# The first unit of the first projection from products of X that is weighted but not normed yet, and seven more convolution taps on TensorE

## The reference

```python
h = rmsnorm(x, norm_mix[0])            # x * rsqrt(mean(x*x) + eps) * g, per token
u = h @ w_pw1 + b_pw1                  # 1024 -> 2048
a, gate = split(u, 2); u = a * sigmoid(gate)
u = causal_depthwise_conv(u, w_dw, width=31) + b_dw
u = silu(layernorm(u, ln_g, ln_b))
x = x + (u @ w_pw2 + b_pw2)
```

## Time and profile before

| | |
|---|---|
| median of 3 runs | 1744.0 us (1743.5 to 1745.08) |
| profiled execution | 1744.05 us |
| its span | 1742.2 us, mean granted TensorE clock 0.996 |
| TensorE busy | 1713.0 us, 98% |
| VectorE busy | 1205.4 us, 69% |
| ACT busy | 833.2 us, 48% |
| GpSimd busy | 273.4 us, 16% |

### The profile page before, as it was taken

How to read it: one execution, slowest core, us unless ns; L and a number is a source line. 1 busy time by engine, 2 the same in 40 slices (tenths; PEclk the granted TensorE clock), 3 DMA queues, 4 the chain that set the end, 5 groups by cost and what they waited for, 6 DMA issues and landing times.

```text
span 1742.2 us, 24232 instructions
## 1 busy us (share of the span) xinstructions
PE 1713.0 (98%) x9506; PEld 1430.2 (82%) x9506; DVE 1205.4 (69%) x1652; ACT 833.2 (48%) x1380; POOL 273.4 (16%) x207
## 2 busy tenths in 40 slices
PE   9999999999999999999999999999999999999998
PEld 6885889889988787799889988766678778888887
DVE  6998789549955555889459956569636676536753
ACT  6876555325633443556226534555654444214432
POOL 2994200000001000200000013672201200000002
PEclk9999999999999999999999999999999999999998
DMA  4210422312231311222412332422112123222321
GB/s 182 95 55 25 127 93 102 137 59 108 98 136 70 129 67 37 93 95 98 157 49 98 118 131 90 146 89 87 61 50 92 68 82 115 91 73 96 107 98 49
DMA packets 28948, 163.45 MB, mean 94 GB/s; under 512 B 4607, under 2 KB 7947, under 8 KB 12460
## 3 DMA queue, kind: packets, MB, share of 16 engines
q1 hardware_dynamic: 25664, 156.28, 25.3%
q10 hardware_dynamic: 3180, 5.74, 1.1%
HBM read 154.65 MB, written 4.47 MB: 91 GB/s over the span
## 4 chain that ended last, share of the span: by engine, by line
PE 84%; DVE 7%; POOL 6%; ACT 2%; issue 1%; DMA 0%; POOLq 0%; ACTq 0%; DVEq 0%
PE PSUM L738 19%; PE PSUM L740 18%; PE PSUM L739 18%; PE PSUM L1007 7%; PE PSUM L1008 7%; PE PSUM L1009 7%; POOL CV L2200 4%; DVE W_lo L2339 1%; POOL ISC L2264 1%; DVE WK L2930 1%; PE PSUM L1243 1%; PE PSUM L1264 1%; PE PSUM L1255 1%; PE PSUM L1094 0%; DVE H_lo L2312 0%
## 5 line engine op out<-in xcount | busy, mean ns | idle before, releaser
L738 PE MATMUL PSUM<-H_hi,W_hi 128*128 128x512 f32 x1056 | 426.0, 403 | 7.7 <-DVE W_lo L2339 2.9
L740 PE MATMUL PSUM<-H_hi,W_lo 128*128 128x512 f32 x1056 | 411.9, 390 | 0.0
L739 PE MATMUL PSUM<-H_lo,W_hi 128*128 128x512 f32 x1056 | 411.9, 390 | 0.0
L1449 ACT ACTIVATE W_hi<-W_raw 128x2048 fp32r<-128x2048 f32 (+1 forms) x96 | 181.9, 1895 | 318.9 <-PE PSUM L740 318.9
L2339 DVE TENSOR_TENSOR W_lo<-W_raw,W_hi 128x2048 fp32r<-128x2048 f32 (+1 forms) x96 | 237.3, 2472 | 71.8 <-ACT W_hi L1449 42.3
L2152 POOL TENSOR_TENSOR SSUM<-SSUM,SQ 128x512 f32<-128x512 f32 x43 | 62.5, 1454 | 1303.6 <-ACT SQ L1516 1301.8
L738 PEld LDWEIGHTS PSUM<-H_hi,W_hi 128*128 128x128 f32 x1056 | 198.3, 188 | 69.3 <-issue 21.2
L740 PEld LDWEIGHTS PSUM<-H_hi,W_lo 128*128 128x128 f32 x1056 | 198.2, 188 | 42.5
L739 PEld LDWEIGHTS PSUM<-H_lo,W_hi 128*128 128x128 f32 x1056 | 198.5, 188 | 37.2 <-issue 1.0
L738 PE MATMUL PSUM<-HID_hi,W_hi 128*128 128x512 f32 x480 | 187.3, 390 | 1.5 <-DVE HID_lo L2504 1.4
L739 PE MATMUL PSUM<-HID_lo,W_hi 128*128 128x512 f32 x480 | 186.8, 389 | 0.0
(11 more groups left out here) (412 smaller groups left out, 3475.5 us busy)
## 6 DMA issues: line engine op xcount, KB each, us to landing
W_raw<-in_inp SPq DMA_DIRECT2D x13, 1024.0 KB, 4.8
W_raw<-in_pw SPq DMA_DIRECT2D x11, 1024.0 KB, 4.8
W_raw<-in_gu0a SPq DMA_DIRECT2D x11, 1024.0 KB, 4.8
W_raw<-in_gu0b SPq DMA_DIRECT2D x11, 1024.0 KB, 4.8
W_raw<-in_gu1a SPq DMA_DIRECT2D x11, 1024.0 KB, 4.8
W_raw<-in_gu1b SPq DMA_DIRECT2D x11, 1024.0 KB, 4.8
W_raw<-in_gu2a SPq DMA_DIRECT2D x11, 1024.0 KB, 4.8
W_raw<-in_gu2b SPq DMA_DIRECT2D x11, 1024.0 KB, 4.8
```

Of the source, the lines that this page charges most:

```text
L738: nc.tensor.matmul(dst[:], wh, x_hi[:, k, :], start=(k == first), stop=False)
L739: nc.tensor.matmul(dst[:], wh, x_lo[:, k, :], start=False, stop=False)
L740: return nc.tensor.matmul(dst[:], wl, x_hi[:, k, :], start=False, stop=(k == last))
L1449: i = nc.scalar.activation(W_hi[b][:, 0:n], W_raw[b][:, 0:n], ACT.Copy)
```

## The change

Unit 0 is no longer split. ACT weights each tile of X with the gain of the norm (`weighted`, the new tensor XG), and TensorE multiplies XG with W_raw directly as fp32 (`whole_product`), from the moment that XG and the weights are in. The sum of squares comes in two parts behind tiles 4 and 5, the spread behind tile 6, and a second spread into AUX[2] behind tile 7, which ACT copies to R. The two banks of unit 0 are multiplied by R on VectorE (`gate_in_place`, `value_in_place`) ahead of the sigmoid and the GLU. For units 1 to 7 the split norm stays, made from XG: tiles 0 to 4 normed by VectorE, tiles 5 to 7 by GpSimd with R. W_hi and W_lo of unit 1 are made ahead of the root, the load of unit 2 waits for the products of unit 0, the loads of X all stand in SP's queue with the halves of W_raw between them, and the loads of pw1 are no loop any more. The tables change: tile 6 goes to TensorE from tap 3 on in place of tap 10 (52 taps become 59), tile 0 has four taps on GpSimd in place of eight, and VectorE has 123 taps in place of 126. `mean_add(2)` moves behind tap 7 of tile 5.

The diff, cut:

```diff
-SS_ADDS = [4, 7, 7, 7, 7, 5, 7, 5]
+SS_ADDS = [6, 7, 7, 7, 7, 5, 7, 5]
...
-COPIED_NORMS = [FFN_PRE, FFN_POST]
+COPIED_NORMS = [MIX0, FFN_PRE, FFN_POST]
...
+WHOLE_UNITS = 1
+POOL_NORMED = 5
+PE_TILES = [(4, 0), (6, 3)]
 PE_TAPS = [(m, t) for m, t0 in PE_TILES for t in range(t0, CONV_WIDTH)]
 PE_ENDS = [n + 1 for n, (m, t) in enumerate(PE_TAPS) if t == CONV_WIDTH - 1]
-DVE_TILES = [(0, 8, CONV_WIDTH), (2, 0, CONV_WIDTH), (3, 0, CONV_WIDTH), (6, 0, 10), (7, 0, CONV_WIDTH)]
-DVE_TAPS = [12] * 7
-POOL_TILES = [(0, 8), (1, CONV_WIDTH), (5, CONV_WIDTH)]
+DVE_TILES = [(0, 4, CONV_WIDTH), (2, 0, CONV_WIDTH), (3, 0, CONV_WIDTH), (6, 0, 3), (7, 0, CONV_WIDTH)]
+DVE_TAPS = [9, 10, 10, 10, 10, 10, 10]
+POOL_TILES = [(0, 4), (1, CONV_WIDTH), (5, CONV_WIDTH)]
 POOL_STEPS = [(m, t) for m, end in POOL_TILES for t in range(end + (end == CONV_WIDTH))]
 POOL_ENDS = [len([x for x in POOL_STEPS if x[0] <= m]) for m, end in POOL_TILES]
 SCALED = [n for n, (m, t) in enumerate(POOL_STEPS) if t >= (1 if m == 0 else 2) and t < CONV_WIDTH]
 CHUNK, CHUNK_BUFS = 6, 4
 CHUNKS = (len(PE_TAPS) + CHUNK - 1) // CHUNK
-PRODUCTS_WITH = [7, 7, 7, 8, 7, 8, 3]
+PRODUCTS_WITH = [3, 7, 7, 8, 7, 8, 3]
...
-MADE = [0, 2, 3, (6, 10), 7, 6]
+MADE = [0, 2, 3, (6, 3), 7, 6]
...
-        ZERO = sb("ZERO", [P, SEQ], at=arena + 26112)
+        ZERO = sb("ZERO", [P, SEQ], at=tail(2))
+        XG = sb("XG", [P, DT, SEQ], at=arena + 17408)
...
+                    if u.i is None and u.c - 2 < WHOLE_UNITS:
+                        sp.wait_ge(acc_ready, 2 * u.c - 2)
...
-            for i in (0, 2):
+            def first_tiles(i):
                 sp.dma_start(X[:, 2 * i:2 * i + 2, :], a["x"][:, 2 * i:2 * i + 2, :]).then_inc(x_in[i], 16)
-            sp.dma_start(vecs[:, 0:DT], a["vecs"][:, 0:DT]).then_inc(gain_in, 16)
+            first_tiles(0)
             sp.dma_start(W_raw[0][:, 0:FIRST_COLS], a["pw1"][0][:, 0:FIRST_COLS]).then_inc(first_in, 16)
+            first_tiles(1)
             sp.dma_start(W_raw[0][:, FIRST_COLS:2 * FIRST_COLS], a["pw1"][0][:, FIRST_COLS:2 * FIRST_COLS]).then_inc(raw_in[0], 16)
+            first_tiles(2)
+            first_tiles(3)
             load(order[0], a["pw1"], At(1))
...
+            def first_sum(part):
+                pe.wait_ge(ss_made, (3, 6)[part])
+                for b in range(4):
+                    last = nc.tensor.matmul(AUX[0][:, b:b + 1], tokens(FIRST_SQ[(0, 4)[part]], b), ones[:, 0:1],
+                                            start=(part == 0 and b == 0), stop=(part == 1 and b == 3))
+                if part:
+                    last.then_inc(stat_ready, 1)
...
+            def whole_product(j, half, k):
+                c = k * COLS + half * P
+                last = nc.tensor.matmul(PS[2 * (j % 2) + half][:], W_raw[j % 2][:, c:c + P], XG[:, k, :], start=(k == 0), stop=(k == L.kt - 1))
+                if k == L.kt - 1:
+                    last.then_inc(acc_ready, 1)
             zero_products(4)
-            pe.wait_ge(const_in, 16)
-            first_sum()
-            zero_products(1)
-            pe.wait_ge(r_made, MIX0 + 1)
-            token_spread(AUX[1], r_ps)
-            zero_products(3)
+            pe.wait_ge(first_in, 16)
             for k in range(L.kt):
-                if k == 0:
-                    pe.wait_ge(first_lo, 1)
                 if k == DT // 2:
-                    pe.wait_ge(w_lo, 1)
+                    pe.wait_ge(raw_in[0], 16)
+                pe.wait_ge(xn_made, k + 1)
+                for half in range(2):
+                    whole_product(0, half, k)
+                if k == 4:
+                    pe.wait_ge(const_in, 16)
+                    first_sum(0)
+                if k == 5:
+                    first_sum(1)
+                if k == 6:
+                    pe.wait_ge(r_made, MIX0 + 1)
+                    token_spread(AUX[1], r_ps)
+            token_spread(AUX[2], r_again)
+            pe.wait_ge(w_lo, 2)
+            for k in range(L.kt):
                 pe.wait_ge(h_lo_made, k + 1)
                 for half in range(2):
-                    last = product(0, L, half, k, H_hi, H_lo)
+                    last = product(1, L, half, k, H_hi, H_lo)
                     if k == L.kt - 1:
                         last.then_inc(acc_ready, 1)
-            for j in range(1, L.n):
+            for j in range(2, L.n):
...
-            act.dma_start(X[:, 2:4, :], a["x"][:, 2:4, :]).then_inc(x_in[1], 16)
+            act.dma_start(vecs[:, 0:DT], a["vecs"][:, 0:DT]).then_inc(gain_in, 16)
             act.dma_start(cmat[:, 0:2, :], a["cmat"][:, 0:2, :]).then_inc(const_in, 16)
-            act.dma_start(X[:, 6:8, :], a["x"][:, 6:8, :]).then_inc(x_in[3], 16)
...
+            def weighted(m):
+                nc.scalar.activation(XG[:, m, :], X[:, m, :], ACT.Copy, scale=vec("norm_mix0", m)).then_inc(xn_made, 1)
             def normed_hi(m):
-                act.wait_ge(xn_made, m + 1)
-                nc.scalar.activation(H_hi[:, m, :], CV[:, m, :], ACT.Copy, scale=vec("norm_mix0", m)).then_inc(h_hi_made, 1)
+                if m < POOL_NORMED:
+                    act.wait_ge(xn_made, DT + m + 1)
+                else:
+                    act.wait_ge(pool_normed, m - POOL_NORMED + 1)
+                nc.scalar.activation(H_hi[:, m, :], CV[:, m, :], ACT.Copy).then_inc(h_hi_made, 1)
             warm_table(ACT.Sqrt)
-            for m in range(DT):
-                if m % 2 == 0:
-                    act.wait_ge(x_in[m // 2], 16)
+            act.wait_ge(gain_in, 16)
+            for m in range(0, DT, 2):
+                act.wait_ge(x_in[m // 2], 16)
+                weighted(m)
+                weighted(m + 1)
                 first_square(m)
+                first_square(m + 1)
+            hi_of(act, At(1), of_unit[1])
             token_std(MIX0)
-            act.wait_ge(first_in, 16)
-            nc.scalar.activation(W_hi[0][:, 0:FIRST_COLS], W_raw[0][:, 0:FIRST_COLS], ACT.Copy).then_inc(w_half, 1)
-            act.wait_ge(gain_in, 16)
-            for m in range(DT):
-                if m == 3:
-                    act.wait_ge(raw_in[0], 16)
-                    nc.scalar.activation(W_hi[0][:, FIRST_COLS:2 * FIRST_COLS], W_raw[0][:, FIRST_COLS:2 * FIRST_COLS],
-                                         ACT.Copy).then_inc(w_hi, 1)
-                normed_hi(m)
-                if m == 5:
-                    hi_of(act, At(1), of_unit[1])
-
             act.wait_ge(vec_in, 16)
             act.dma_start(cmat[:, 2:4, :], a["cmat"][:, 2:4, :]).then_inc(const2_in, 16)
-
+            warm_table(ACT.Sigmoid)
             nc.scalar.activation(tap_hi[:], vecs[:, vec_at["w_dw"]:vec_at["w_dw"] + CONV_WIDTH * DT], ACT.Copy).then_inc(w_parts, 1)
+            normed_hi(0)
+            act.wait_ge(r_again, 1)
+            nc.scalar.activation(R[:], AUX[2][:], ACT.Copy).then_inc(r_copied, 1)
+            for m in range(1, DT):
+                normed_hi(m)
...
+                if j < WHOLE_UNITS:
+                    act.wait_ge(glu_in, j + 1)
+                    src = GATE[j % 2]
+                else:
+                    act.wait_ge(acc_ready, 2 * j + 2)
+                    src = PS[2 * (j % 2) + 1]
                 if j >= 2:
                     act.wait_ge(glu_made, j - 1)
-                nc.scalar.activation(GATE[j % 2][:], PS[2 * (j % 2) + 1][:], ACT.Sigmoid, bias=vec("b_pw1", At(DT + j))).then_inc(gate_act, 1)
+                nc.scalar.activation(GATE[j % 2][:], src[:], ACT.Sigmoid, bias=vec("b_pw1", At(DT + j))).then_inc(gate_act, 1)
...
+            split_hi(act, L, At(0))
             for j in range(L.n):
                 glu_gate(j)
                 if j < L.n - 1:
-                    split_hi(act, L, At(j))
+                    if j:
+                        split_hi(act, L, At(j))
...
+            pool.wait_ge(r_copied, COPIED_NORMS.index(MIX0) + 1)
+            for m in range(POOL_NORMED, DT):
+                pool.wait_ge(xn_made, m + 1)
+                if m > POOL_NORMED:
+                    pool.wait_ge(pool_normed, m - POOL_NORMED)
+                nc.gpsimd.tensor_tensor(CV[:, m, :], XG[:, m, :], R[:], ALU.mult).then_inc(pool_normed, 1)
...
+                    if (m, t) == (5, 8):
+                        mean_add(2)
...
-            mean_add(2)
...
+            def first_pair(k):
                 dve.wait_ge(sq_made, 2 * k + 2)
                 nc.vector.tensor_tensor(FIRST_SQ[2 * k], FIRST_SQ[2 * k], FIRST_SQ[2 * k + 1], ALU.add).then_inc(ss_made, 1)
+            def two_pairs(k, made):
+                dve.wait_ge(ss_made, made)
+                nc.vector.tensor_tensor(FIRST_SQ[2 * k], FIRST_SQ[2 * k], FIRST_SQ[2 * k + 2], ALU.add).then_inc(ss_made, 1)
+            def normed(m):
+                nc.vector.tensor_tensor(CV[:, m, :], XG[:, m, :], AUX[1][:], ALU.mult).then_inc(xn_made, 1)
+            def normed_lo(m):
+                dve.wait_ge(h_hi_made, m + 1)
```

(93 more changed lines are left out.)

20 lines of the change are left out of this document (9 added, 11 removed).

## The result

The changed kernel takes 1748.26 us (median of 13 runs, 1747.85 to 1749.04), the kernel before 1744.14 in the same sessions (13 runs, 1743.5 to 1745.37): ratio 1.0023, interval 1.0015 to 1.0031. It is slower, by 4.1 us, and 1748.0 was forecast. The profiled execution took 1748.37 us.

The account below looks back on a forecast made before the run. It took the later of TensorE's and GpSimd's trains to bound the first stage: UP_lo 1.0 us earlier, 4.9 us for seven taps, so +3.9 at the LayerNorm sum; span 1746.1 plus 1.85 gives 1748.0 us, range 1743.8 to 1750.0.

Parts of the forecast that it names:

- GpSimd's train: GpSimd's taps up to conv_lo(1): gains 1.0 us, UP_lo of tile 6 starts at 127.3 and releases TensorE at 128.7.
- What bounds it: First stage: the later of TensorE's and GpSimd's nearly level trains sets the taps of tile 6; TensorE would stand 3.4 us.
- TensorE's start: Unit 0 as 16 fp32 products from 6.6 us, 13.8 us plus 3.8 between; unit 1 starts at 24.1, 7.0 us won.
- Unit 1: Second projection unit on TensorE: stalls of 2.7 us in all behind the norms, ends at 37.7; unit 2 starts at 38.2.
- The turns: GpSimd's three norms and VectorE's H_lo alternate at the shared ports from 25.2; without them unit 1 ends at 35.9.
- the rival of shorter turns: In the norms of unit 1: no or shorter turns, UP_lo 3.1 us earlier than before, +1.8, 1745.9 us; chance 0.22.
- a scaled add of tile 1 well before 49: Sign of being wrong, on GpSimd: its first scaled add of tile 1, forecast at 49.3, coming well before 49.
- the wait on UP_lo: Sign ahead of the taps of tile 6: TensorE waits some 3.4 us if right, no wait if wrong.
- Seven taps: Taps of tile 6 added to TensorE: 0.71 us a tap, 4.9 us for seven.
- Edits at nothing: Edits priced at zero under cover: VectorE's taps end at 146, GpSimd near 148.5; diagonals made by 140; loads wait as before.
- GpSimd not being what holds TensorE: At the taps of tile 6: only TensorE's train counts, +0.6 to -2.6, 1741.5 to 1744.7 us; chance 0.13.
- The late start: At unit 0: W_raw at 7.7 instead of 6.6, or one more GpSimd turn; 1749.0 to 1750.4 us; chance 0.10.

Follow-up runs that it names:

- the first experiment: Changed kernel with one line moved: conv_lo(1), which makes UP_lo of tile 6, ahead of tap 14 of tile 5 instead of tap 18; 1744.62 us.
- the second experiment: Changed kernel with the seven taps of tile 6 back on VectorE (TensorE from tap 10); 1745.89 us.
- the fourth experiment: Changed kernel with three fp32 products of constants into a free bank just ahead of TensorE's wait on UP_lo of tile 6; 1748.01 us.
- the repeat: The changed kernel as it is, measured again in the second set; 1748.12 us, ratio 1.0018 to the kernel before.

## Why the prediction came out right

The time was 0.3 us off, with the mechanism as forecast, but two terms of the sum were wrong and nearly cancelled: GpSimd's train was put 1.06 us too late, and 1.54 us of low clock was left out. That these two cancelled is luck. The train that holds TensorE, the wait and the price of the taps came out for the reasons given.

**What bounds it: right.** The later of two trains, TensorE's and GpSimd's, sets the taps of tile 6, and GpSimd's is it, as the wait of 3.10 us shows (3.4 forecast). Taking it away gave 4.84 us (the first experiment).

**TensorE's start: right.** Unit 1 at 24.16 against 24.1, the first norm at 21.91 against 21.7. Ten fp32 products take 15.52 - 6.93 = 8.6 us by the profile, 0.86 each as the LayerNorm sum's row gave. Here too two small errors offset each other: unit 0 started 0.33 later than the 6.6 forecast (6.93), and the two sums and two spreads took 3.5 us in place of 3.8.

**Unit 1: right in kind, too dear.** I had stalls of 1.6, 0.55 and 0.55. Measured from where the next product would have followed, they are 27.06 - 25.62 = 1.44, and 0.2 and 0.2; each first product behind a stall also takes 0.11 longer. The unit took 13.22 us and not 13.6. The turns exist: the Trainium skill's exclusive lock (SBUF — State Buffer, Who interferes with whom) agrees with 1.41 and 1.18 in place of 0.69. But a round of one GpSimd norm and one H_lo is 28.63 - 26.93 = 1.70 us and not 1.3 + 0.6. VectorE reached W_lo of unit 2 at 34.99 and not 35.8, and it ended at 37.27 and not 38.1; unit 2 started at 37.38, not 38.2.

**GpSimd's train: the first wrong term.** I had it gain 1.0 us. It gained 2.06 (48.22 against 50.28), because the turns' 0.8 and about 0.1 a step pass on undiminished: GLU at 43.11 and not 44.1, first scaled add at 48.22 and not 49.3. What I had carried over from before (2.2 us from the end of W_lo to that add; the train from there) kept its size, 46.04 to 48.22 and 78.08. This is half of the way to the rival of shorter turns. By it alone the time would have been 1746.9. The prediction had named "a scaled add of tile 1 well before 49" as a sign of being wrong, and 48.22 is such a sign for this term; the wait on UP_lo, its other sign, stayed.

**Seven taps: right.** 4.9 forecast, 4.88 by the second experiment against the changed kernel.

**What a wait costs: the missing term.** I priced the wait at its length. It also dropped the clock for 3.3 us, 1.54 by the second experiment and 1.58 by the fourth. The wait of before, 0.42, and the one of 0.52 in the fourth experiment did not. 1748.0 - 1.06 + 1.54 = 1748.5, and the execution took 1748.37. The Trainium skill has the behaviour (TensorE: Matmul & The Clock Gate, What's actually happening): an idle array falls back to 1.2 GHz and has to work before it rises. The trace agrees, with 0.52 behind the wait; the prediction has no term for it and names no such rival.

**Edits at nothing: right.** VectorE ended at 143.9 and GpSimd at 147.6, ahead of 151.15, 2 and 1 us earlier than forecast.

**The rivals.** GpSimd not being what holds TensorE would have needed another 3 us; the first experiment made that case by hand and came to 1744.62, at the top of the range given for it (1741.5 to 1744.7). The late start did not come in the profiled execution; in the repeat unit 0 started 0.8 later, at 7.73, and that execution took 1750.46, but only 0.7 us of that is the start.
